# A decoder trunk of four layers on one core: the 520 token columns split at 256 instead of 260

## What is computed

```python
def short_conv_mixer(x, buf, w_in, conv_w, w_out):
    b_gate, c_gate, xi = jnp.split(x @ w_in, 3, axis=-1)
    y, new_buf = causal_dwconv(c_gate * xi, buf, conv_w)
    return (b_gate * y) @ w_out, new_buf

def conv_ffn(x, buf, w_up, conv_w, conv_b, w_down):
    h_gate, h_val = jnp.split(x @ w_up, 2, axis=-1)
    hc, new_buf = causal_dwconv(h_gate, buf, conv_w)
    return (jax.nn.silu(hc + conv_b) * h_val) @ w_down, new_buf

for l in range(DEPTH):          # mod holds shift, scale and gate of each sub-layer
    u = rmsnorm(h, g[l, 0]) * (1 + sc_m) + sh_m
    out = mixer[l % 3](u, ...)
    h = h + gt_m * rmsnorm(out, g[l, 1])
    u = rmsnorm(h, g[l, 2]) * (1 + sc_f) + sh_f
    out = conv_ffn(u, ...)
    h = h + gt_f * rmsnorm(out, g[l, 3])
```

## Time and profile before

| | us |
|---|---|
| three runs | 3500.45, 3500.97, 3511.65 |
| median | 3500.97 |
| the profiled execution, its own time | 3498.4 |
| its span, first to last instruction | 3496.7 |
| TensorE busy in it | 3151.7 |
| VectorE / GpSimd / ScalarE busy | 1582.4 / 1314.5 / 1093.3 |

### The profile page before, as it was taken

How to read it: one execution, slowest core, us unless ns; L and a number is a source line. 1 busy time by engine, 2 the same in 40 slices (tenths; PEclk the granted TensorE clock), 3 DMA queues, 4 the chain that set the end, 5 groups by cost and what they waited for, 6 DMA issues and landing times. The chain is left out here.

```text
span 3496.7 us, 78105 instructions
## 1 busy us (share of the span) xinstructions
PE 3151.7 (90%) x30651; PEld 2916.3 (83%) x30651; DVE 1582.4 (45%) x2423; ACT 1093.3 (31%) x2124; POOL 1314.5 (38%) x910
## 2 busy tenths in 40 slices
PE   7998999958979997889999896778999989989997
PEld 5997999937968885789998694667999979989997
DVE  3336663083047774276621203436664044376622
ACT  3224332243242222243322326124332232243321
POOL 3343444434312332334443231233444324434442
PEclk8998999969969999789999897688999989989998
DMA  7532334503510001123344352022334535323332
GB/s 241 157 121 64 89 92 142 159 20 120 151 37 3 3 3 47 55 63 89 91 151 147 99 157 80 4 76 67 91 91 129 162 103 159 113 62 91 91 89 79
DMA packets 527398, 330.80 MB, mean 95 GB/s; under 512 B 19786, under 2 KB 519448, under 8 KB 526946
## 3 DMA queue, kind: packets, MB, share of 16 engines
q1 hardware_dynamic: 517912, 317.63, 30.1%
q10 hardware_dynamic: 9322, 10.77, 1.0%
HBM read 318.57 MB, written 10.20 MB: 94 GB/s over the span
## 5 line engine op out<-in xcount | busy, mean ns | idle before, releaser
L601 POOL TENSOR_TENSOR w_lo<-w_raw,w_hi 128x1024 fp32r<-128x1024 f32 x406 | 1025.3, 2526 | 1202.6 <-ACT w_hi L770 1202.6
L1339 PE MATMUL bank<-u_hi,w_hi 128*128 128x260 f32 (+1 forms) x4240 | 879.2, 289 | 47.0 <-ACT w_hi L770 23.3
L1339 PE MATMUL bank<-u_lo,w_hi 128*128 128x260 f32 (+1 forms) x4240 | 863.9, 285 | 0.0
L1339 PEld LDWEIGHTS bank<-u_hi,w_hi 128*128 128x128 f32 (+1 forms) x4240 | 654.7, 189 | 81.9 <-issue 49.4
L1339 PEld LDWEIGHTS bank<-u_lo,w_hi 128*128 128x128 f32 (+1 forms) x4240 | 659.2, 189 | 1.8
L770 ACT ACTIVATE w_hi<-w_raw 128x1024 fp32r<-128x1024 f32 x406 | 428.9, 1056 | 489.5 <-PE bank L1345 224.0
L1345 PE MATMUL bank<-u_hi,w_lo 128*128 128x260 f32 (+1 forms) x4240 | 551.8, 283 | 0.0
L1345 PEld LDWEIGHTS bank<-u_hi,w_lo 128*128 128x128 f32 (+1 forms) x4240 | 525.3, 187 | 1.3
L1339 PE MATMUL bank<-hid_hi,w_hi 128*128 128x260 f32 x1664 | 342.9, 287 | 0.0
L1339 PE MATMUL bank<-hid_lo,w_hi 128*128 128x260 f32 x1664 | 335.1, 283 | 0.0
L1339 PEld LDWEIGHTS bank<-hid_hi,w_hi 128*128 128x128 f32 x1664 | 256.2, 188 | 28.5 <-issue 28.4
(11 more groups left out here) (383 smaller groups left out, 4187.7 us busy)
## 6 DMA issues: line engine op xcount, KB each, us to landing
w_raw<-in_ffn_w_up_dram SPq DMA_DIRECT2D x176, 512.0 KB, 3.7
ada_raw<-in_ada_w_dram SPq DMA_DIRECT2D x168, 512.0 KB, 3.5
w_raw<-in_ffn_w_down_dram SPq DMA_DIRECT2D x64, 448.0 KB, 4.2
w_raw<-in_sconv_w_in_dram SPq DMA_DIRECT2D x48, 512.0 KB, 4.6
w_raw<-in_ffn_w_down_dram SPq DMA_DIRECT2D x32, 512.0 KB, 4.6
ada_pro<-in_ada_w_dram SPq DMA_DIRECT2D x6, 2048.0 KB, 20.5
w_raw<-in_rwkv_w_rkv_dram SPq DMA_DIRECT2D x24, 512.0 KB, 4.5
w_raw<-in_gla_w_in_dram SPq DMA_DIRECT2D x24, 512.0 KB, 4.6
```

Of the source, the lines that this page charges most:

```text
L601: pool.tensor_tensor(w_lo[:, s, :, :], w_raw[:, s, :, :], w_hi[:, s, :, :].bitcast(F32), ALU.subtract).then_inc(lo_done, 1)
L1339: pe.matmul(tile_ps[slot][half][0:width, 0:HALF], w_hi[:, s, k, 0:width], x[:, k0 + k, half * HALF:(half + 1) * HALF], start=start and k = ...
```

## The change

The halves become unequal: half 0 has the columns 0 to 255, half 1 the columns 256 to 519, 264 of them. Two helpers give the columns of a half in the activation and in its PSUM bank, and all products, copies and operations that work on a half use them or `T - HALF`. In `gemm` the parameter width is renamed cols. Copies that end at the prompt's last token (TP - HALF columns) go from 252 to 256 columns; the 8 sample columns stay a copy of their own. The diff below is cut to one example of each kind; the places left out are `square_last`, `lora_tile`, `gate_rank`, the gate of GLA (L991), the sigmoids of RWKV (L1086), `gemm_pair`, the fp32 products at L1554, L1830, L1837 and L1853, the gate in sconv (L2091) and the operations of VectorE at L2410, L2417 and L2443, all edited in the same way.

```diff
-HALF = T // 2
+HALF = 256
...
+def half_cols(half):
+    return slice(HALF, T) if half else slice(0, HALF)
+
+
+def half_width(half):
+    return slice(0, T - HALF if half else HALF)
...
             def evacuate(t_half, s, n, dst):
 
                 act.wait_ge(block_done, n + 3)
                 act.activation(dst[:, 0:HALF], tile_ps[s][0][:, 0:HALF], ACT.Copy)
-                return act.activation(dst[:, HALF:T], tile_ps[s][1][:, 0:HALF], ACT.Copy)
+                return act.activation(dst[:, HALF:T], tile_ps[s][1][:, 0:T - HALF], ACT.Copy)
...
                         act.activation(gate[:, e, 2:2 + HALF], tile_ps[0][0][:, 0:HALF], ACT.Copy)
                         act.activation(gate[:, e, 2 + HALF:2 + TP], tile_ps[0][1][:, 0:TP - HALF], ACT.Copy)
-                        act.activation(gate[:, e, TP + 4:GW:3], tile_ps[0][1][:, TP - HALF:HALF], ACT.Copy)\
+                        act.activation(gate[:, e, TP + 4:GW:3], tile_ps[0][1][:, TP - HALF:T - HALF], ACT.Copy)\
                            .then_inc(gate_ready, 1)
...
-            def gemm(n, s, slot, xh, xl, k0, nk, start, stop, ready=None, width=P, mix=0):
+            def gemm(n, s, slot, xh, xl, k0, nk, start, stop, ready=None, cols=P, mix=0):
...
                         for half in range(2):
-                            pe.matmul(tile_ps[slot][half][0:width, 0:HALF], w_hi[:, s, k, 0:width],
-                                      x[:, k0 + k, half * HALF:(half + 1) * HALF],
+                            pe.matmul(tile_ps[slot][half][0:cols, half_width(half)], w_hi[:, s, k, 0:cols],
+                                      x[:, k0 + k, half_cols(half)],
                                       start=start and k == 0 and i == 0, stop=False)
                 pe.wait_ge(lo_done, n + 3)
                 for k in range(nk):
                     for half in range(2):
-                        mm = pe.matmul(tile_ps[slot][half][0:width, 0:HALF], w_lo[:, s, k, 0:width],
-                                       xh[:, k0 + k, half * HALF:(half + 1) * HALF], start=False, stop=stop and k == nk - 1)
+                        mm = pe.matmul(tile_ps[slot][half][0:cols, half_width(half)], w_lo[:, s, k, 0:cols],
+                                       xh[:, k0 + k, half_cols(half)], start=False, stop=stop and k == nk - 1)
                 return mm.then_inc(block_done, 1)
...
                             for half in range(2):
-                                mm = pe.matmul(tile_ps[slot][half][:, 0:HALF], lora2[:, slot, k * P:(k + 1) * P],
-                                               t_lora[:, slot, half * HALF:(half + 1) * HALF], start=True, stop=True)
+                                mm = pe.matmul(tile_ps[slot][half][:, half_width(half)], lora2[:, slot, k * P:(k + 1) * P],
+                                               t_lora[:, slot, half_cols(half)], start=True, stop=True)
...
                 dve.tensor_tensor(prod[:, e, 0:HALF], conv[:, e, 0:HALF], tile_ps[slot][0][:, 0:HALF], ALU.mult)
                 dve.tensor_tensor(prod[:, e, HALF:TP], conv[:, e, HALF:TP], tile_ps[slot][1][:, 0:TP - HALF], ALU.mult)
-                dve.tensor_tensor(prod[:, e, TP:T], conv[:, e, TP + 2:CWD:3], tile_ps[slot][1][:, TP - HALF:HALF],
+                dve.tensor_tensor(prod[:, e, TP:T], conv[:, e, TP + 2:CWD:3], tile_ps[slot][1][:, TP - HALF:T - HALF],
                                   ALU.mult).then_inc(tile_free[slot], 1)
```

More of the change, by code:

```diff
@@ L1359, in gemm_pair @@
                             for half in range(2):
-                                pe.matmul(tile_ps[s][half][:, 0:HALF], w[:, s, k, :],
-                                          xh[:, k, half * HALF:(half + 1) * HALF], start=(k == 0 and i == 0), stop=False)
+                                pe.matmul(tile_ps[s][half][:, half_width(half)], w[:, s, k, :],
+                                          xh[:, k, half_cols(half)], start=(k == 0 and i == 0), stop=False)
                     pe.wait_ge(ready[0], ready[1] + k + 1)
@@ L1364, in gemm_pair @@
                         for half in range(2):
-                            mm = pe.matmul(tile_ps[s][half][:, 0:HALF], w_hi[:, s, k, :],
-                                           xl[:, k, half * HALF:(half + 1) * HALF], start=False, stop=(k == KT - 1))
+                            mm = pe.matmul(tile_ps[s][half][:, half_width(half)], w_hi[:, s, k, :],
+                                           xl[:, k, half_cols(half)], start=False, stop=(k == KT - 1))
                         if k == KT - 1:
@@ L1507, in _ @@
                         pe.wait_ge(tile_free[k % 2], t0 // 2 + k // 2 + 1)
-                        gemm(n0 + k, k % 2, k % 2, *x, 0, KT, True, True, x_ready, width=HD, mix=o)
+                        gemm(n0 + k, k % 2, k % 2, *x, 0, KT, True, True, x_ready, cols=HD, mix=o)
                     pe.wait_ge(tile_free[1], t0 // 2 + 2)
-                    gemm(n0 + 3, 1, 1, u_hi, u_lo, 0, KT, True, True, width=HD)
+                    gemm(n0 + 3, 1, 1, u_hi, u_lo, 0, KT, True, True, cols=HD)
                     pe.wait_ge(urows_copied, 1)
@@ L1532, in _ @@
                         gemm(n0 + k, k, k, u_hi, u_lo, 0, KT, True, True,
-                             (u_ready, KT * (p["split"] - 1)) if k == 0 else None, width=8)
+                             (u_ready, KT * (p["split"] - 1)) if k == 0 else None, cols=8)
                     def in_pair(it, first=False):
@@ L1829, in _ @@
                             for half in range(2):
-                                mm = pe.matmul(tile_ps[0][half][:, 0:HALF], pair_ones[:, :],
-                                               rw_y[:, k, half * HALF:(half + 1) * HALF], start=True, stop=True)
+                                mm = pe.matmul(tile_ps[0][half][:, half_width(half)], pair_ones[:, :],
+                                               rw_y[:, k, half_cols(half)], start=True, stop=True)
                             mm.then_inc(mean_mm, 1)
@@ L1836, in _ @@
                             for half in range(2):
-                                mm = pe.matmul(ss_ps[half][:, 0:HALF], pair_ones[:, :],
-                                               rw_r[:, k, half * HALF:(half + 1) * HALF], start=True, stop=True)
+                                mm = pe.matmul(ss_ps[half][:, half_width(half)], pair_ones[:, :],
+                                               rw_r[:, k, half_cols(half)], start=True, stop=True)
                             mm.then_inc(bonus_mm, 1)
@@ L1852, in _ @@
                             for i in range(2):
-                                mm = pe.matmul(bank[4 + 2 * (k % 2) + half][:, 0:HALF], g2[:, i, k * P:(k + 1) * P],
-                                               t_g[:, i, half * HALF:(half + 1) * HALF], start=(i == 0),
+                                mm = pe.matmul(bank[4 + 2 * (k % 2) + half][:, half_width(half)], g2[:, i, k * P:(k + 1) * P],
+                                               t_g[:, i, half_cols(half)], start=(i == 0),
                                                stop=(i == 1))
```

32 lines of the change are left out of this document (16 added, 16 removed).

## The result

The changed kernel took 3515.86 us in the median of 20 runs (3503.89 to 3520.43), the kernel before 3500.92 us in 20 runs beside them (3496.84 to 3514.54). The ratio is 1.0031, 95% interval 1.0020 to 1.0041: 0.3% slower, as much as the prediction said a measurement can just tell from no change. The means, 3514.3 and 3504.5 us, lie 9.8 us apart. The time lies in the predicted range (3464 to 3518), but 15 us above the forecast of 3501 and outside the 3490 to 3511 that the likeliest case gave itself. It is also almost exactly what rival C had priced (3517), and that is the first thing that has to be cleared up.

What follows compares the result with a forecast made beforehand. TensorE's own products were taken as the bound. Product pairs and other edits each added 0 us to the profiled 3498, and the forecast was given on the three-run median: 3501 us, range 3464 to 3518 for 8 in 10.

Steps and rivals of the forecast that it cites:

- the likeliest case: All split products: pairs cost the same, change 0 us, 3501 us with its own range 3490 to 3511; chance 0.52.
- rival C: Block products: a floor keeps the 256-column product at 119.5 ns while the 264-column one pays: +16 us, 3517 us; chance 0.10.
- What bounds the kernel: Whole kernel: the products are bound by TensorE itself, busy 90% of 3496.7 us; waits are next to nothing beside that.
- Either is a + b x columns, and then a pair costs the same: Product pairs: fixed cost plus columns, 239 ns before and after, 0 us; bounded by -107 and +107 us.
- A: Operand reads: begun 32- or 64-byte stretches count whole, so the split saves 32 us, giving 3469 us; chance 0.26.
- B: 256-column products: they lose all or half of 11.2 ns, saving 53 to 107 us, 3394 to 3448 us; chance 0.09.
- the surplus: Block products at full clock: 119.5 ns each, 11.2 ns over the 108.3 ns of a column-by-column count.
- Rival D: 256-column products: they leave the one-cycle mode, 433 instead of 118 ns, over 3 ms more; chance 0.03 with other losses.
- how many instructions the split touches: Block products: 19,104 of 260 columns, 9,552 pairs; nothing added or removed, no load or DMA moved, no wait changed.
- would mean a wait that I take as untouched: Sign of error: pair unchanged at 239 ns, yet the kernel's time moves over 10 us.
- PE busy 3152 us within 10: Sign in the changed profile: TensorE's busy time over the whole kernel if the forecast is right.
- within 0.3%: Whole kernel: time the same within what a measurement can tell, 0.3% (10 us); chance 0.52, faster 0.35, slower 0.13.

Runs made afterwards that it cites:

- experiments 11 and 12: The changed kernel cut at 224 and 296 columns, then at 200 and 320, each run twice: 3600.3 us (ratio 1.0266) and 3685.8 us (1.0510).
- the first job: The first 20 runs of the changed kernel beside the kernel before: 3515.9 us, ratio 1.0031.
- the 85 unchanged runs: The kernel before, unedited, run beside the experiments, three of 88 runs left out: mean 3503.7 us at clock 0.9228.
- the second job, changed again: The changed kernel, not edited further, run 12 more times beside the kernel before: 3507.7 us, ratio 1.0011.
- six kernels: Six kernels with block products split off the middle, the changed one again among them, 62 runs against 108 with those at 260: 7.3 ± 1.8 us longer.
- the mixers': The kernel before with only the sconv, rproj, gproj and out products split at 256, all else at 260: 3509.1 us, ratio 1.0021.
- 252 + 268: The changed kernel with its halves cut at 252 and 268 columns: 3506.0 us, ratio 1.0016.
- with fillers: Both kernels with unread products of constants where TensorE waits: the kernel before 3511.9 us (ratio 1.0020), the changed one 3516.3 us (1.0033).
- rest 256: The changed kernel with only the halves of RWKV's group norm and gate back at 260 columns: 3512.7 us, ratio 1.0026.
- 264 + 256: The changed kernel with the long half first, 264 columns and then 256: 3512.8 us, ratio 1.0028.
- the ConvFFN's: The kernel before with only the ConvFFN's up and down products and readers split at 256, all else at 260: 3512.9 us, ratio 1.0028.
- 224 + 296: The changed kernel with its halves cut at 224 and 296 columns, two runs: 3600.3 us, ratio 1.0266.
- norm 256: The kernel before with only the halves of RWKV's group norm and gate at 256 and 264 columns: 3504.4 us, ratio 0.9998.

## Why the prediction was right or wrong

**"What bounds the kernel": right.** Work on the width of the products moved the time by the full count of them: 9.5 and 18.5 ns a pair in experiments 11 and 12 came through in the whole kernel, as they should if the prediction's 19,104 products are on the path.

**"Either is a + b x columns, and then a pair costs the same": right, to 0.3 ns.** The singles came at 118.2 and 121.2 ns where 117.8 and 121.2 were forecast; the pair is 239.2 before and 239.5 after, by the starts of all pairs at full clock. The term that was set to 0 is +2.9 us by these, with +4.1 ± 1.3 measured on runs at equal clock. Its bounds of -107 and +107 us were far too wide.

**Rivals A and B: refuted.** No pair is shorter than before at any of the five splits, so neither begun stretches nor an odd width explain the surplus. What does is open. Half 1 began on or 32 bytes past a multiple of 64 with the splits at 256 and 264, and 16 or 48 past one with 252, and the pairs of these kernels cost the same within 0.4 ns. The Trainium skill (page "SBUF — State Buffer", Specifications) lets lines of 16 bytes cost something as they begin; the sum of 64 + 66 is that of 65 + 65, and by that rule nothing is gained, with which these runs agree. The rule that the prediction took from the Trainium skill ("TensorE: Matmul & The Clock Gate", Back-to-back issue gap), N/2.4 + 2.5 ns, is called there the gap of an isolated product, with no room for a weight load. Its slope is 0.417 ns a column, near the 0.45 measured, and at 256 columns it gives an estimate of 109.2 ns, where the trace has 118.2: it is some 9 ns short from 252 to 268 columns.

**Rival C: right in kind, wrong in place, and its price met the result by chance.** It gave 3517 us and the median was 3515.86. Had the comparison ended there, C would have passed for proven. But it says that the 256-column product stays at 119.5 and the pair becomes 241, and the trace has 118.2 and 239.5. The floor exists, where loads would follow each other in under 108 ns, and the change doesn't reach it. The condition in the prediction ("it decides if the floor lies above 117.8") was the right one to ask, and the answer is no. The trace of the kernel before held it already: some of its loads of 128 weight columns begin 108 ns after the one before, so at 119.5 ns the loads were not yet at their closest. What the prediction set against it, that 64 weight columns left 119.4 ns, says the same more weakly.

**Rival D: refuted** down to 200 columns, the narrowest tried: no product there takes anything near 433 ns.

**The step that failed** is the last one of "how many instructions the split touches" and of what would prove the forecast wrong: with the pair unchanged, a move of over 10 us "would mean a wait that I take as untouched". The pair is unchanged, the time moved 15 us in the first job, and no wait did it (56.5 and 29.7 us in the two longest against 56.2 and 28.7). The sum had no term for the granted clock. The clock stood in the earlier trace rows, read as a label of the stages, while it differs from run to run of the same kernel and takes 2.7 us with every 0.001. Of the 10.6 us by which the changed kernel's mean is above that of the 85 unchanged runs, 6.5 go with the clock and 4.1 stand at equal clock. In the second job it was 1.9 and 4.2. The forecast of "PE busy 3152 us within 10" fell by the same: 3167.3 in one execution of the changed kernel, 3158.0 in another, and 3162.2 in the second trace of the kernel before. That a pair's price was set to exactly 0 is the lesser miss, 2.9 us.

**The chances** put "within 0.3%" first. That was right for what the pairs cost: +0.1%, at equal clock or by their starts. The whole effect on the time is more, +0.2% (7.3 ± 1.8 us) over six kernels with such a split, and half of it is a lower clock, for which no case in the list stood. The first job's 0.31% is above that mean, the second's 0.11% below. That the time still fell into the range from 3464 to 3518 is owed to rival C, whose price held its upper end up, and not to the mechanism that took it there.

**What stays open.** Why the clock is lower, and whether it is the split as such. For it: the sum over six kernels above, and the changed kernel (0.9204) and the mixers' (0.9206) with the lowest means of all that ran more than twice. Against: 252 + 268 has 0.9227, and the changed kernel itself had 0.9221 when run again, where the kernel before, run again, has 0.9223; and with fillers the two kernels have the same clock. The traces show something small and regular. In two places where the products of a down stage have ended and TensorE works in short groups, all three traces of kernels with every block product split at 256 (changed, changed again, rest 256) have 3.4 us more at half clock than both traces of the kernel before. The kernel before:

```profile
2815.00:2865.00 50.00, 33.20 (x285) 26.49 (x284) 34.40 (x72) 23.14 (x38) 7.42 (x5) 0.75 0.22 65
3466.00:3496.00 30.00, 8.99 (x72) 7.66 (x70) 15.77 (x33) 4.56 (x10) 0.00 (x0) 0.71 0.18 71
```

and the same work of the changed kernel, second trace (7 us later):

```profile
2822.00:2872.00 50.00, 34.16 (x279) 28.11 (x279) 35.00 (x73) 22.84 (x35) 8.14 (x6) 0.72 0.23 71
3473.00:3503.00 30.00, 9.06 (x64) 7.77 (x58) 15.78 (x33) 4.56 (x10) 0.00 (x0) 0.66 0.18 71
```

By matched starts this is 1.4 and 1.0 us of time. In the first place most of it comes back: the next piece at half clock is shorter by the same 3.4 us, and from 2790 to 2880 the traces of both kernels have 30.7 us at half clock, and changed again and rest 256 are 0.2 us behind the first trace of the kernel before (the first trace of the changed kernel 1.0). At the end of the kernel the 1.0 us stays. It goes with no one part of the change: 252 + 268 and 264 + 256 have it in the first place alone, the ConvFFN's, the mixers' and 224 + 296 at the end of the kernel alone, norm 256 in neither. Why, no run here says; in the long stretches with gaps (1345 to 1460, 2110 to 2300) the clock differs as much between two executions of one kernel as between the two kernels.

## What to carry to other kernels

Before a difference of a few tenths of a per cent is explained from two traces, compare the granted clock of the runs, and if it differs, set the times against it: here 2.7 us for 0.001 makes up 6.5 of 10.6 us, and 12 more runs of the unchanged kernel cost less than a wrong theory. A forecast for such a kernel should carry that scatter as a term of its range, and a lower clock as a possible effect of the change itself. And moving a split of 520 columns off the middle, as far as 252 + 268, costs 0.3 to 0.6 ns a pair and gains nothing, because a product costs nearly a + b x columns there; below some 245 columns (an estimate) the load of 128 weight columns sets a floor, and alignment of the halves to 64 bytes buys nothing.

## What was not expected of the hardware

- Loads of 128 weight columns never begin less than 108 ns apart, in any of five traces. When a short product would need them closer, the pair gets dearer: with 224 columns by 9.5 ns, with 200 by 18.5 ns.
- Two products of unequal width are dearer than two of equal width by 0.3 to 0.6 ns a pair already at 252 to 268 columns, where the loads are 116 ns apart and more in the mean of a stage.
- The same kernel on one core ran at a mean granted clock of 0.918 to 0.926 from one execution to the next, and its time, which follows the clock, spread over 3496 to 3516 us.
- Filling TensorE's gaps with idle products raised the clock from 0.923 to 0.926 and cut the scatter from 5.8 to 2.6 us in the kernel before, and still cost 8 us net.
